# Two small products turned round, and a modulation sum moved, in a ten-stage block on one core

## The chip, the cores and the metric

The kernel runs on one core of a Trainium2 chip. The metric is device time in microseconds (us). The engines are TensorE (PE; its weight loads are PEld), VectorE (DVE), ScalarE (ACT), GpSimd (POOL, unused here) and SyncE (SP), which issues most DMAs.

## The reference, cut to what matters

A sequence of 256 tokens of width 1024 goes through ten stages: ffn, mamba, ffn, ffn, moba, ffn, sb, cffn, dsa, cffn. Each begins with an RMSNorm whose shift, scale and gate come from a vector product with the condition `c` (adaLN):

```python
m = c_act @ w + b
shift, scale, gate = jnp.split(m, 3, axis=-1)
h = rmsnorm(x, g) * (1.0 + scale[:, None, :]) + shift[:, None, :]
x = x + g * y
```

The Mamba stage needs, beside its wide projection, 32 columns of `h @ w_in`, one for each head: `dt = softplus(dt + dt_bias)`. Its cumulative sums set the decays between tokens. The sparse attention (dsa) needs 8 columns of `h @ w_in`, the weights `wi` of the index heads; a token's index score is the sum over heads of `wi` times the relu of a product of index query and index key, and the best 256 keys are kept.

## The kernel before

`x` is kept transposed in SBUF, 8 tiles of 128 channels x 256 tokens. Everything is computed at better than one-pass precision: each operand is split into a part rounded to a short format (`w_hi`, `h_hi`, type fp32r) and the rest (`w_lo`, `h_lo`), and `three` issues three matmuls, hi x hi, hi x lo and lo x hi (L1365 to L1367). Weights come as 277 blocks of 128x2048. For each block SyncE loads `raw` (a ring of six), ScalarE rounds it to `w_hi` (L420) and VectorE subtracts (`w_lo`, L816); these two are called `split`, and they run two blocks ahead of TensorE. A block is used up by `gemm` (48 products of 256 columns into one PSUM bank: two halves `m` of 24) or by `gemm_out` and `last` (into the accumulators, banks 0 to 3).

Each engine has its own program, a hand-written order of instructions; engines wait for one another only through counted semaphores, `k.wait(name, stage)` and `k.inc(name, instruction)`. A waiting instruction holds back all that stands behind it on its engine.

The small weights, 8 tiles of 128x40 (32 columns for Mamba, 8 for dsa), are in `ws_hi` and `ws_lo`. In the Mamba stage TensorE does, for the first group of heads: the first block into bank 4; `timestep`; the second block into bank 5 (B and C); the third into bank 7 (z); `cum` (L1517 to L1523, the cumulative sums of dt x a); then transposes and scores. `timestep` has h as weights (128 channels x 128 tokens) and the 32 small columns as moving operand: 2 halves of tokens x 8 tiles x 3 products, 48 in all. The result stands with tokens on partitions, as VectorE's `timestep` (L1055 to L1071, softplus) wants it, in bank 6, columns 0 to 63. VectorE has before it in its queue a `split` and the conv taps of the first block (L1095); ScalarE does four of the steps in between (L538 to L543).

In dsa `sparse_front` does: the block of latent and index keys into bank 4; 48 products with 8 columns into bank 7; the product for the relative bias (`relp`, L1765) into bank 7; two more blocks (index queries) into banks 5 and 6, with a ones product for a norm between them (L1772); two transposes (L1775); then index scores for eight heads (L1782, L1783), which VectorE sums with the `wi` weights (L1308). VectorE's copy `relv` (L1294) lets ScalarE store the bias and go on to its next `split`.

The adaLN sums: during earlier ffn stages VectorE has multiplied and summed the modulation weights (`gather`, `fold`). At a stage's end `last` does the last block in four pairs of tiles. After each pair VectorE's `residual` adds to `x` (L949, and for Mamba L945 before it; a `split` stands between pairs 1 and 2), ScalarE squares (L436), and TensorE sums the squares over partitions for the next norm (`squares`, L1423, fp32, two passes each). `modulation` on TensorE (L1415, one product of 96 columns with the `fold` matrix) stands between `squares` 1 and 2 of the tail; `modulation` on VectorE (four sums L874 and two or three small steps, L886 to L889) stands behind `residual`. The next norm waits for `rstd` and for it (L907).

Of the kernel before, what the change touches and what calls it, by code (L numbers as in the profile page):

```python
# [23 lines left out]
ALU = mybir.AluOpType  # L24
# [3 lines left out]
P = 128  # L28
T = 256
# [93 lines left out]
class Plan:  # L123
# [20 lines left out]
    def steps(self, st, kind):  # L144
        g = GROUPS[kind]
        out = {"fold": 4, "mods": 1, "modv": 1, "pair": 3, "xup": 8, "sq": 8, "ss": 1, "ln": 1, "rstd": 1,
               "t": 8, "hhi": 8, "hlo": 8, "zero": 1, "ahi": 0, "alo": 0}
        if st == RESCALED:
            out |= {"sq": 16, "ln": 2, "rstd": 2, "ms2": 4, "xfin": 8}
        if kind in ("ffn", "cffn"):  # L150
            out |= {"silu": g, "mul": g, "ahi": g, "alo": g}
        if kind == "cffn":
            out |= {"cid": 2 * g, "tap1": 2 * g, "tap2": 2 * g}
        if kind == "mamba":
            out |= {"dtp": 1, "dta": 12, "dtx": 4, "acp": 1, "acv": 3, "sq0": 1, "cid": 2 * g, "tap": 6 * g,
                    "sil": 3 * g, "acg": g, "xt": g, "cb": g, "br": 4 * g, "xdt": g, "cbs": g, "dx": g,
                    "dec": 4 * g, "wv": 4 * g, "yc": g, "y1": g, "zw": g, "yz": g, "ysq": g, "yn": g, "yac": g,
                    "ahi": g, "alo": g, "rs2p": 1, "rs2": 2, "xr": 8}
        if kind in ("moba", "sb", "dsa"):
            out |= {"sc": 4 * g, "qev": g, "lg": 4 * g, "ptp": 4 * g, "ptc": 4 * g, "pv": 2 * g,  # L160
                    "ahi": 2 * g, "alo": 2 * g}
        if kind in ("moba", "sb"):
            out |= {"kev": g, "vev": g}
        if kind in ("moba", "dsa"):
            out |= {"mx": 4 * g, "nm": 4 * g, "ex": 4 * g, "rc": 4 * g, "prs": 4 * g}
        if kind == "sb":
            out |= {"ab": 4 * g, "ea": 4 * g, "la": 4 * g, "lk": 4 * g, "prb": 4 * g, "arg": 4 * g}
        if kind == "dsa":
            out |= {"qev2": g, "pre": 3, "wip": 1, "relp": 1, "wiv": 1, "relv": 1, "ix": 8, "rel": 8,
                    "isc": 10, "top": 32, "msk": 2, "ksq": 1, "kss": 1, "klr": 2, "gkq": 1, "kn": 1,  # L170
                    "ltp": 1, "ltc": 1, "qsq": 2 * g, "qss": g, "qlr": 2 * g, "ol": 2 * g, "olc": 2 * g, "wu": g}
        return out
# [35 lines left out]
def build(nc, weights, mods, params, consts, xin, out, stages=None):  # L208
# [3 lines left out]
    with ExitStack() as ctx:  # L212
# [94 lines left out]
        dta = mix[:, 5696:5824].rearrange("p (a d h) -> p a d h", a=2, d=2)  # L307
        ea = mix[:, 5824:5856]
        r2 = mix[:, 5856:6112]
        yn = work[:, 1536:2048].rearrange("p (a t) -> p a t", a=2)  # L310

        Q = view(0, 4, T)
# [484 lines left out]
        def _(eng):  # L797
# [242 lines left out]
            def mamba(st):  # L1040
# [2 lines left out]
                step = [0]  # L1043

                def timestep():
                    k.wait("dtp", st)

                    def dt_step(ins, wait=True):
                        k.inc("dta", ins)
                        step[0] += 1  # L1050
                        if wait:
                            k.wait("dta", st, b=step[0] - 1)


                    dt_step(eng.tensor_tensor(dv.rearrange("p (a h) -> p a h", a=2),  # L1055
                                              bank[6][:, 0:64].rearrange("p (a h) -> p a h", a=2),
                                              par_("dtb").unsqueeze(1).to_broadcast([P, 2, 32]), ALU.add), False)
                    k.wait("dtx", st, b=1)
                    dt_step(eng.tensor_scalar(dw, de, 1.0, None, ALU.add))
                    k.wait("dtx", st, b=2)  # L1060
                    dt_step(eng.tensor_scalar(dw, dw, 1.0, None, ALU.subtract))
                    dt_step(eng.tensor_scalar(dm, dw, 0.0, None, ALU.is_equal))
                    dt_step(eng.tensor_tensor(dw, dw, dm, ALU.add))
                    dt_step(eng.reciprocal(dw, dw))
                    dt_step(eng.tensor_tensor(dl, dl, dm, ALU.add))
                    dt_step(eng.tensor_tensor(dl, dl, dw, ALU.mult))
                    dt_step(eng.tensor_tensor(dl, dl, de, ALU.mult))
                    dt_step(eng.scalar_tensor_tensor(out=dtt, in0=dv, scalar=0.0, in1=dl, op0=ALU.max, op1=ALU.add))
                    k.wait("dtx", st, b=3)
                    for d in range(2):  # L1070
                        dt_step(eng.scalar_tensor_tensor(  # L1071
                            out=dta[:, :, d, :], in0=dtt.rearrange("p (a h) -> p a h", a=2),
                            scalar=-1.0, in1=ea.unsqueeze(1).to_broadcast([P, 2, 32]), op0=ALU.mult, op1=ALU.mult), False)
# [214 lines left out]
            def sparse_front(st):  # L1288

                split(st, b=0)  # L1290
                k.wait("relp", st)
                k.inc("wiv", eng.tensor_scalar(wi, bank[7][:, 0:16].rearrange("p (a h) -> p a h", a=2), 8 ** -0.5,
                                               None, ALU.mult))
                k.inc("relv", eng.tensor_copy(relS, bank[7][0:16, P:512]))  # L1294
                k.inc("gkq", eng.tensor_tensor(gkq, par_("qn"), par_("kn"), ALU.mult))
                k.inc("isc", eng.memset(isc, 0.0))
                split(st, b=1)
                k.wait("gkq", st)
                k.wait("klr", st, b=1)
                k.inc("kn", eng.scalar_tensor_tensor(out=kn, in0=latT, scalar=gkq, in1=rstd[:, :],  # L1300
# [44 lines left out]
            for st, kind in enumerate(stages):  # L1345
                norm(st)
                programs[kind](st)
                residual(st)
                if st + 1 < NST:
                    modulation(st + 1)  # L1350


        @block.tensor
        def _(eng):
# [11 lines left out]
                eng.matmul(dst, ah, bl, start=False, stop=False, skip_group_check=skip)  # L1366
                return eng.matmul(dst, al, bh, start=False, stop=stop, skip_group_check=skip)  # L1367

            def gemm(dst, st, i=0, a=0, b=0, tokens=False, first=False):

                hi, lo = [w.rearrange("p (k n) -> p k n", k=KT) for w in begin(st, i, a, b)]
                both = [(m, slice(m * P, (m + 1) * P), dst[:, m * T:(m + 1) * T]) for m in range(2)]
# [13 lines left out]
                                            skip_group_check=True)  # L1386
                else:
                    for m, part, d in both:
                        for kk in range(KT):
                            if tokens:  # L1390
                                mm = three(d, h_hi[:, kk, part], h_lo[:, kk, part], hi[:, kk, :], lo[:, kk, :],
                                           kk == 0, kk == KT - 1)
                            else:
                                mm = three(d, hi[:, kk, part], lo[:, kk, part], h_hi[:, kk, :], h_lo[:, kk, :],
                                           kk == 0, kk == KT - 1)
# [75 lines left out]
            def last(st, ready):  # L1471
# [6 lines left out]
                if st == 0:  # L1478
                    eng.wait_ge(sems["go"], KT + 2)
                    eng.matmul(bank[7][:, 96:128], con_("fold"), gfold, start=True,  # L1480
                               stop=True).then_inc(sems["gmods"], 1)
                for pair in range(4):
                    if pair == 3 and more:
                        squares(st + 1, 0)
# [8 lines left out]
                        mm.then_inc(sems["blk"], 1)  # L1493
                if more:
                    squares(st + 1, 1)
                    modulation(st + 1)
                    squares(st + 1, 2)
                    squares(st + 1, 3)

            def mamba(st):  # L1500
                def timestep():
                    k.wait("rstd", st)
                    for tt in range(2):
                        for kk in range(KT):
                            part = slice(tt * P, (tt + 1) * P)
                            ws = slice(40 * kk, 40 * kk + 32)
                            mm = three(bank[6][:, 32 * tt:32 * tt + 32], h_hi[:, kk, part], h_lo[:, kk, part],
                                       ws_hi[:, ws], ws_lo[:, ws], kk == 0, kk == KT - 1)
                    k.inc("dtp", mm)

                tri, ones = con_("tri"), con_("ones")
# [57 lines left out]
                def body(i, a, b):  # L1569
# [5 lines left out]
                    else:  # L1575
                        timestep()
                    k.wait("cbs", st, i, 1, -1)
                    gemm(bank[5], st, i, a, b + 1)
                    if more:
                        y_out(i)  # L1580
                        k.wait("dec", st, i, 4, -1)
# [173 lines left out]
            def sparse_front(st):  # L1755
                gemm(bank[4], st, b=0, first=True)
                k.wait("modv", st)
                for tt in range(2):
                    for kk in range(KT):
                        part, ws = slice(tt * P, (tt + 1) * P), slice(40 * kk + 32, 40 * kk + 40)  # L1760
                        mm = three(bank[7][:, 8 * tt:8 * tt + 8], h_hi[:, kk, part], h_lo[:, kk, part],
                                   ws_hi[:, ws], ws_lo[:, ws], kk == 0, kk == KT - 1)
                k.inc("wip", mm)
                o, _ = PARAMS["relb"]
                k.inc("relp", eng.matmul(bank[7][0:16, P:512], par[0:32, o:o + 16], con_("onehot", 32),  # L1765
                                         start=True, stop=True))
                for n in (1, 2):
                    gemm(bank[4 + n], st, b=n)
                    if n == 1:
                        k.wait("relv", st)  # L1770
                        k.wait("ksq", st)
                        k.inc("kss", eng.matmul(bank[7][:, 0:T], con_("ones"), qsq[0][:, 0:T], start=True, stop=True))  # L1772
# [131 lines left out]
```

## Time and profile before

| what | us |
|---|---|
| runs | 1894.99, 1885.89, 1892.75; median 1892.75 |
| profiled execution, its own time | 1896.41 |
| its span from first to last instruction | 1894.6 |
| TensorE matmuls busy | 1795.6 (95%) |
| TensorE weight loads busy | 1737.1 (92%) |
| VectorE busy | 1445.1 (76%) |
| ScalarE busy | 961.7 (51%) |
| mean granted TensorE clock | 0.982 |

Matmuls are pipelined: each record is longer than the distance to the next start, so a pace is read from the starts. A granted clock of 1.00 is 2.4 GHz, 0.50 is 1.2 GHz.

### The profile page before, as it was taken

How to read it: one execution, taken by the hardware profiler on the slowest of the kernel's cores; microseconds unless marked ns; L12 is line 12 of the kernel's file. 1: busy time of each engine (PE TensorE's matmuls, PEld its weight loads, DVE VectorE, ACT ScalarE, POOL GpSimd, SP SyncE). 2: the span in 40 equal slices, each digit the busy share in tenths (PEclk: the TensorE clock that was granted, in tenths of full speed). 3: DMA queues.
4: the chain of work that ended last, by engine and by line, in shares of the span. 5: the costliest groups of instructions: out<-in, count | busy, mean ns of one | idle time of the engine just before them, and what ended most of it. 6: DMA issues, size and time to landing. Idle time of an engine off the chain costs nothing.

```text
span 1894.6 us, 34144 instructions
## 1 busy us (share of the span) xinstructions
PE 1795.6 (95%) x14644; PEld 1737.1 (92%) x14644; DVE 1445.1 (76%) x1716; ACT 961.7 (51%) x1256; POOL 0.2 (0%) x4
## 2 busy tenths in 40 slices
PE   2998999999999999999989999898999999989999
PEld 2998989998999999999979999897999988979999
DVE  7799877877789878976548897655898667447666
ACT  3433456666543454346564444555644555666553
POOL 0000000000000000000000000000000000000000
PEclk9999999999999999999999999999999998999999
DMA  9998824343599759973426996232485544324551
GB/s 399 417 366 340 300 109 156 135 177 134 187 380 365 309 218 371 361 296 130 178 101 262 347 393 250 109 140 109 175 320 192 181 142 161 118 90 162 193 180 42
DMA packets 67278, 426.11 MB, mean 225 GB/s; under 512 B 7264, under 2 KB 10352, under 8 KB 30448
## 3 DMA queue, kind: packets, MB, share of 16 engines
q1 hardware_dynamic: 63216, 415.21, 57.9%
q10 hardware_dynamic: 3968, 9.63, 1.5%
q8 instruction: 61, 1.00, 0.2%
q14 instruction: 33, 0.27, 0.0%
HBM read 423.74 MB, written 3.17 MB: 225 GB/s over the span
## 4 chain that ended last, share of the span: by engine, by line
PE 85%; DVE 10%; ACT 3%; issue 1%; DMA 1%; SPq 0%; DVEq 0%; ACTq 0%
PE bank L1365 24%; PE bank L1367 24%; PE bank L1366 24%; DVE w_lo L816 3%; PE bank L1423 2%; DVE macc L847 2%; DMA modws<-mods 1%; PE bank L1687 1%; PE bank L1378 1%; PE bank L1380 1%; DVE mix L1002 1%; PE bank L1385 1%; PE bank L1529 1%; PE bank L1668 1%; PE bank L1564 0%
## 5 line engine op out<-in xcount | busy, mean ns | idle before, releaser
L1365 PE MATMUL bank<-h_hi,w_hi 128*128 128x256 f32 x2864 | 810.4, 283 | 14.0 <-DVE w_lo L816 12.3
L1366 PE MATMUL bank<-h_lo,w_hi 128*128 128x256 f32 x2864 | 804.4, 281 | 0.0
L1367 PE MATMUL bank<-h_hi,w_lo 128*128 128x256 f32 x2864 | 804.2, 281 | 0.0
L816 DVE TENSOR_TENSOR w_lo<-raw,w_hi 128x2048 fp32r<-128x2048 f32 x277 | 633.4, 2288 | 128.1 <-ACT w_hi L420 127.6
L420 ACT ACTIVATE w_hi<-raw 128x2048 fp32r<-128x2048 f32 x277 | 529.3, 1911 | 155.8 <-PE bank L1367 144.5
L1365 PEld LDWEIGHTS bank<-h_hi,w_hi 128*128 128x128 f32 x2864 | 543.8, 190 | 19.5 <-DVE w_lo L816 15.1
L1366 PEld LDWEIGHTS bank<-h_lo,w_hi 128*128 128x128 f32 x2864 | 546.7, 191 | 0.2
L1367 PEld LDWEIGHTS bank<-h_hi,w_lo 128*128 128x128 f32 x2864 | 545.3, 190 | 0.0
L1365 PE MATMUL bank<-a_hi,w_hi 128*128 128x256 f32 x1280 | 362.4, 283 | 3.1 <-DVE a_lo L1244 3.1
L1366 PE MATMUL bank<-a_lo,w_hi 128*128 128x256 f32 x1280 | 359.6, 281 | 0.0
L1367 PE MATMUL bank<-a_hi,w_lo 128*128 128x256 f32 x1280 | 359.2, 281 | 0.0
L1365 PEld LDWEIGHTS bank<-a_hi,w_hi 128*128 128x128 f32 x1280 | 241.7, 189 | 6.0 <-issue 5.2
L1366 PEld LDWEIGHTS bank<-a_lo,w_hi 128*128 128x128 f32 x1280 | 241.6, 189 | 0.2
L1367 PEld LDWEIGHTS bank<-a_hi,w_lo 128*128 128x128 f32 x1280 | 241.7, 189 | 0.0
L847 DVE SCALAR_TENSOR_TENSOR macc<-modws,cact,macc 128x1536 f32<-128x1536 f32 x126 | 226.3, 1814 | 0.0
L1002 DVE SCALAR_TENSOR_TENSOR mix<-bank,par,mix 128x254 f32<-128x254 f32 (+1 forms) x176 | 76.7, 478 | 49.5 <-ACT mix L495 47.9
L470 ACT ACTIVATE a_hi<-mix 128x512 fp32r<-128x512 f32 x40 | 25.3, 633 | 154.1 <-PE bank L1367 124.8
L456 ACT ACTIVATE mix<-bank 128x512 f32<-128x512 f32 x44 | 26.4, 600 | 121.5 <-PE bank L1367 121.5
L495 ACT ACTIVATE mix<-bank,par 128x256 f32<-128x256 f32 x88 | 44.8, 559 | 84.0 <-PE bank L1367 83.9
L1423 PE MATMUL bank<-work,con 128*128 128x256 f32 x160 | 42.9, 399 | 32.2 <-DMA con<-consts 31.2
L1423 PEld LDWEIGHTS bank<-work,con 128*128 128x128 f32 x160 | 29.7, 200 | 36.1 <-DMA con<-consts 31.2
L968 DVE TENSOR_TENSOR a_lo<-mix,a_hi 128x512 fp32r<-128x512 f32 x40 | 27.7, 692 | 42.1 <-ACT a_hi L470 42.1
(250 smaller groups left out, 1692.4 us busy)
## 6 DMA issues: line engine op xcount, KB each, us to landing
raw<-weights SPq DMA_DIRECT2D x277, 1024.0 KB, 4.9
modws<-mods SPq DMA_DIRECT2D x144, 768.0 KB, 6.5
mix<-mods SPq DMA_DIRECT2D x6, 1024.0 KB, 8.1
mix<-mods ACTq DMA_DIRECT2D x8, 512.0 KB, 10.3
modws<-mods SPq DMA_DIRECT2D x2, 1024.0 KB, 12.1
biases<-scratch ACTq DMA_DIRECT2D x1, 2048.0 KB, 12.2
mix<-biases ACTq DMA_DIRECT2D x4, 512.0 KB, 4.2
par<-params ACTq DMA_DIRECT2D x1, 1189.0 KB, 8.3
```

What stands on the lines that cost most here:

```text
L420: eng.activation(w_hi[g % NW][:, :], raw[g % NRAW][:, :], ACT.Copy).then_inc(sems["whi"], 1)
L456: k.inc("silu", eng.activation(sg, bank[4][:, :].rearrange("p (a t) -> p a t", a=2), ACT.Silu))
L470: k.inc("ahi", eng.activation(z_hi if final else a_hi[:, :, :], act, ACT.Copy))
L495: ins = eng.activation(dst[:, m, :], b[:, m * T:(m + 1) * T], ACT.Identity, scale=cw(i, t, 2), bias=cw(i, t, 3))
L816: eng.tensor_tensor(w_lo[g % NW][:, :], raw[g % NRAW][:, :], w_hi[g % NW][:, :], ALU.subtract).then_inc(sems["wlo"], 1)
L847: ins = eng.scalar_tensor_tensor(out=m, in0=modw[q % 4], scalar=c, in1=m, op0=ALU.mult, op1=ALU.add)
L968: k.inc("alo", eng.tensor_tensor(z_lo if final else a_lo[:, :, :], act, z_hi if final else a_hi[:, :, :], ALU.subtract))
L1002: ins = eng.scalar_tensor_tensor(out=dst[:, m, lag:T], in0=b[:, m * T:(m + 1) * T - lag], scalar=cw(i, 22 * up + m, tap), in1=dst[:, m, la ...
L1365: eng.matmul(dst, ah, bh, start=start, stop=False, skip_group_check=skip)
L1366: eng.matmul(dst, ah, bl, start=False, stop=False, skip_group_check=skip)
L1367: return eng.matmul(dst, al, bh, start=False, stop=stop, skip_group_check=skip)
L1423: mm = eng.matmul(bank[6][:, r * T:(r + 1) * T], con_("ones"), (sq2 if r else work3)[:, m, :], start=m == r == 0, stop=m == KT - 1, skip_g ...
```

## The change

Three edits. The Mamba time step has the small columns as weights and h as moving operand: 8 x 3 = 24 products of 256 columns give 32 rows (heads) x 256 tokens; VectorE copies them to SBUF (`dtrow`, semaphores `dtr`, `dtc`); two transposes on TensorE, put between the two halves of the second block, bring them back to tokens on partitions, in bank 6 from column 256 on. The index weights of dsa are done likewise: 24 products give 8 rows in bank 6, VectorE copies them (`wirow`), two transposes stand behind the second block, and the scaled copy `wi` (`wiv`) moves behind VectorE's second split; the third block, which writes bank 6, waits for it. `modulation` of the next stage moves, on TensorE from the tail to the head of `last` (behind `ready`), and on VectorE ahead of `residual`.

```diff
@@ VectorE, Mamba
                 def timestep():
+                    k.wait("dtr", st)
+                    k.inc("dtc", eng.tensor_copy(dtrow, bank[6][0:32, 0:T]))
                     k.wait("dtp", st)
...
-                                              bank[6][:, 0:64].rearrange("p (a h) -> p a h", a=2),
+                                              bank[6][:, T:T + 64].rearrange("p (a h) -> p a h", a=2),
@@ VectorE, sparse_front
                 split(st, b=0)
+                k.wait("wir", st)
+                k.inc("wic", eng.tensor_copy(wirow, bank[6][0:8, 0:T]))
                 k.wait("relp", st)
-                k.inc("wiv", eng.tensor_scalar(wi, bank[7][:, 0:16].rearrange("p (a h) -> p a h", a=2), 8 ** -0.5,
-                                               None, ALU.mult))
...
                 split(st, b=1)
+                k.wait("wip", st)
+                k.inc("wiv", eng.tensor_scalar(wi, bank[6][:, T:T + 16].rearrange("p (a h) -> p a h", a=2), 8 ** -0.5,
+                                               None, ALU.mult))
@@ VectorE, stages
                 programs[kind](st)
-                residual(st)
                 if st + 1 < NST:
                     modulation(st + 1)
+                residual(st)
@@ TensorE, gemm
                     for m, part, d in both:
+                        if m and between:
+                            between()
@@ TensorE, last
+                if more:
+                    modulation(st + 1)
                 for pair in range(4):
...
                 if more:
                     squares(st + 1, 1)
-                    modulation(st + 1)
                     squares(st + 1, 2)
@@ TensorE, Mamba
                 def timestep():
                     k.wait("rstd", st)
+                    for kk in range(KT):
+                        ws = slice(40 * kk, 40 * kk + 32)
+                        mm = three(bank[6][0:32, 0:T], ws_hi[:, ws], ws_lo[:, ws], h_hi[:, kk, :], h_lo[:, kk, :],
+                                   kk == 0, kk == KT - 1)
+                    k.inc("dtr", mm)
+
+                def timestep_columns():
+                    k.wait("dtc", st)
                     for tt in range(2):
-                        for kk in range(KT):
-                            part = slice(tt * P, (tt + 1) * P)
-                            ws = slice(40 * kk, 40 * kk + 32)
-                            mm = three(bank[6][:, 32 * tt:32 * tt + 32], h_hi[:, kk, part], h_lo[:, kk, part],
-                                       ws_hi[:, ws], ws_lo[:, ws], kk == 0, kk == KT - 1)
+                        mm = eng.transpose(bank[6][:, T + 32 * tt:T + 32 * tt + 32], dtrow[:, tt * P:(tt + 1) * P],
+                                           con_("ident")[0:32, 0:32])
                     k.inc("dtp", mm)
...
-                    gemm(bank[5], st, i, a, b + 1)
+                    gemm(bank[5], st, i, a, b + 1, between=None if more else timestep_columns)
@@ TensorE, sparse_front
-                for tt in range(2):
-                    for kk in range(KT):
-                        part, ws = slice(tt * P, (tt + 1) * P), slice(40 * kk + 32, 40 * kk + 40)
-                        mm = three(bank[7][:, 8 * tt:8 * tt + 8], h_hi[:, kk, part], h_lo[:, kk, part],
-                                   ws_hi[:, ws], ws_lo[:, ws], kk == 0, kk == KT - 1)
-                k.inc("wip", mm)
+                for kk in range(KT):
+                    ws = slice(40 * kk + 32, 40 * kk + 40)
+                    mm = three(bank[6][0:8, 0:T], ws_hi[:, ws], ws_lo[:, ws], h_hi[:, kk, :], h_lo[:, kk, :],
+                               kk == 0, kk == KT - 1)
+                k.inc("wir", mm)
...
                 for n in (1, 2):
+                    if n == 2:
+                        k.wait("wiv", st)
                     gemm(bank[4 + n], st, b=n)
                     if n == 1:
+                        k.wait("wic", st)
+                        for tt in range(2):
+                            mm = eng.transpose(bank[6][:, T + 8 * tt:T + 8 * tt + 8], wirow[:, tt * P:(tt + 1) * P],
+                                               con_("ident")[0:8, 0:8])
+                        k.inc("wip", mm)
                         k.wait("relv", st)
```

`dtrow` is `work[0:32, 1536:1792]` and `wirow` is `work[0:8, 0:256]`.

## Rows read from the trace of the kernel before

**Rows 1.** The page: span, and the chain that ended last by engine.
```profile
span 1894.6 us, 34144 instructions
...
PE 85%; DVE 10%; ACT 3%; issue 1%; DMA 1%; SPq 0%; DVEq 0%; ACTq 0%
```
**Rows 2.** Timeline of PE, Mamba stage: start us, duration us, what.
```profile
246.57 0.26 PE L1366 MATMUL bank<-ws_lo,h_hi 128*128 128x32 f32 x1
...
250.70 0.33 PE L1367 MATMUL bank<-ws_hi,h_lo 128*128 128x32 f32 x1
...
252.78 0.56 PE L1365 MATMUL bank<-h_hi,w_hi 128*128 128x256 f32 x1
...
257.73 0.28 PE L1367 MATMUL bank<-h_hi,w_lo 128*128 128x256 f32 x1
...
265.90 0.28 PE L1367 MATMUL bank<-h_hi,w_lo 128*128 128x256 f32 x1
```
**Rows 3.** Windows: stretch, length, busy us (records) of PE, PEld, DVE, ACT, POOL, clock, DMA.
```profile
246.50:250.80 4.30, 4.30 (x41) 4.30 (x40) 4.20 (x7) 1.02 (x2) 0.00 (x0) 1.00 0.19 38
252.80:257.40 4.60, 4.60 (x22) 4.60 (x23) 3.14 (x13) 3.85 (x6) 0.00 (x0) 0.50 0.04 16
283.50:286.70 3.20, 3.20 (x32) 2.79 (x31) 2.65 (x6) 2.82 (x3) 0.00 (x0) 1.00 0.37 113
1543.70:1547.70 4.00, 4.00 (x39) 4.00 (x38) 1.77 (x1) 1.07 (x3) 0.00 (x0) 1.00 0.35 66
1551.60:1554.40 2.80, 2.80 (x14) 2.80 (x14) 1.07 (x4) 1.61 (x1) 0.00 (x0) 0.50 0.04 9
```
**Rows 4.** Timeline of DVE, Mamba stage: taps, first and last softplus step, a copy from PSUM.
```profile
248.78 2.69 DVE L1095 SCALAR_TENSOR_TENSOR mix<-bank,par,mix 128x255 f32<-128x255 f32 x6
252.98 0.23 DVE L1055 TENSOR_TENSOR mix<-bank,par 128x64 f32<-128x64 f32 x1 [1.52 <-PE bank L1367]
...
256.75 0.36 DVE L1071 SCALAR_TENSOR_TENSOR mix<-mix 128x64 f32<-128x64 f32 x2
...
267.74 0.41 DVE L1080 CAST acg<-bank 64x256 fp32r<-64x256 f32 x1
```
**Rows 5.** Timeline of PE, dsa front: first and last small product, bias product, next block.
```profile
1543.74 0.17 PE L1365 MATMUL bank<-ws_hi,h_hi 128*128 128x8 f32 x1
...
1549.91 0.35 PE L1367 MATMUL bank<-ws_hi,h_lo 128*128 128x8 f32 x1
1550.19 1.46 PE L1765 MATMUL bank<-con,par 32*16 32x384 f32 x2
1551.58 0.58 PE L1365 MATMUL bank<-h_hi,w_hi 128*128 128x256 f32 x1
```
**Rows 6.** Timeline of PE, dsa front: the ones product in fp32 and two transposes.
```profile
1558.59 0.59 PE L1772 MATMUL bank<-work,con 128*128 128x256 f32 x2
...
1564.67 0.38 PE L1775 MATMUL bank<-con,mix 128*128 128x128 f32 x2
```
**Rows 7.** Timeline of DVE, dsa front: the copy of the bias and the next split.
```profile
1551.78 0.53 DVE L1294 COPY mix<-bank 16x384 f32<-16x384 f32 x1
...
1554.73 2.29 DVE L816 TENSOR_TENSOR w_lo<-raw,w_hi 128x2048 fp32r<-128x2048 f32 x1 [1.95 <-ACT w_hi L420]
```
**Rows 8.** Timeline, end of the fourth stage (ffn): squares, modulation, next norm.
```profile
863.37 1.02 PE L1423 MATMUL bank<-work,con 128*128 128x256 f32 x4
...
864.23 0.36 PE L1415 MATMUL bank<-folded,con 128*128 128x96 f32 x2
...
864.43 1.92 PE L1423 MATMUL bank<-work,con 128*128 128x256 f32 x8
864.63 0.75 DVE L874 TENSOR_TENSOR modv<-bank,par 32x24 f32<-32x24 f32 x4
...
867.34 0.88 DVE L907 SCALAR_TENSOR_TENSOR work<-x,gs,rstd 128x256 f32<-128x256 f32 x2 [1.55 <-ACT rstd L426]
```
**Rows 9.** Timeline of PE, end of the Mamba stage: the last squares.
```profile
483.23 1.13 PE L1423 MATMUL bank<-work,con 128*128 128x256 f32 x4 [0.69 <-ACT work L436]
...
484.69 1.13 PE L1423 MATMUL bank<-work,con 128*128 128x256 f32 x4 [0.32 <-ACT work L436]
```

More of the change, by code:

```diff
@@ L154, in steps @@
         if kind == "mamba":
-            out |= {"dtp": 1, "dta": 12, "dtx": 4, "acp": 1, "acv": 3, "sq0": 1, "cid": 2 * g, "tap": 6 * g,
+            out |= {"dtr": 1, "dtc": 1, "dtp": 1, "dta": 12, "dtx": 4, "acp": 1, "acv": 3, "sq0": 1, "cid": 2 * g, "tap": 6 * g,
                     "sil": 3 * g, "acg": g, "xt": g, "cb": g, "br": 4 * g, "xdt": g, "cbs": g, "dx": g,
@@ L168, in steps @@
         if kind == "dsa":
-            out |= {"qev2": g, "pre": 3, "wip": 1, "relp": 1, "wiv": 1, "relv": 1, "ix": 8, "rel": 8,
+            out |= {"qev2": g, "pre": 3, "wir": 1, "wic": 1, "wip": 1, "relp": 1, "wiv": 1, "relv": 1, "ix": 8, "rel": 8,
                     "isc": 10, "top": 32, "msk": 2, "ksq": 1, "kss": 1, "klr": 2, "gkq": 1, "kn": 1,
@@ L309, in build @@
         r2 = mix[:, 5856:6112]
+        dtrow, wirow = work[0:32, 1536:1792], work[0:8, 0:256]
         yn = work[:, 1536:2048].rearrange("p (a t) -> p a t", a=2)
@@ L1367, in three, with gemm @@
                 return eng.matmul(dst, al, bh, start=False, stop=stop, skip_group_check=skip)
-            def gemm(dst, st, i=0, a=0, b=0, tokens=False, first=False):
+            def gemm(dst, st, i=0, a=0, b=0, tokens=False, first=False, between=None):
                 hi, lo = [w.rearrange("p (k n) -> p k n", k=KT) for w in begin(st, i, a, b)]
```

## The prediction

> **What bounds the kernel now.** I read the page first: the chain that ended last is matmul for 85% of a span of 1894.6 us [rows 1]. So a microsecond taken out of TensorE's stream counts in full wherever TensorE is the last to arrive, and the views that matter are TensorE's timeline at the places that the diff touches, then the granted clock there (windows), then VectorE and ScalarE around them, to see whether they can follow an earlier TensorE.
>
> The diff touches two stretches of small products and the ends of nine stages. Both small stretches lie on the chain: TensorE has no gap in them. In the Mamba stage the 48 products with 32 columns start every (250.70 - 246.57) / 37 = 0.1117 us [rows 2], while the big products just behind them, with 256 columns, start every (265.90 - 257.73) / 72 = 0.1135 us at full clock [rows 2]. Eight times the columns at the same pace: what paces the small product is not its moving side; its 128x128 weight load is the only thing that it has in common with the big one. And the clock: it is granted in full up to 250.8 us, 1.00 in the windows view, and is at half from about 250.8 to 257.4 us, 0.50 [rows 3], that is 1.2 instead of 2.4 GHz, though TensorE was never idle. The same happens behind the 8-column products of the DSA stage, 1.00 until 1547.7 us and 0.50 in the stretch from 1551.6 us [rows 3]. What went before the fall both times is some 4 us of products that stream 32 or 8 columns in the time of 256.
>
> **Part one, Mamba time step.** Before, from 246.53 (one start ahead of the first row of [rows 2]) to the cumulative products at 266.01 (the last product starts at 265.90, one pace before them [rows 2]): 19.48 us. These are 48 small products, 6.25 us, of which 48 x 0.1117 = 5.36 is the pace and 0.89 the low clock; and 96 big ones, 13.23 us from 252.78, of which 96 x 0.1135 = 10.90 is the pace and 2.33 the low clock.
>
> After: 24 products with 256 moving columns of h and 32 weight columns. No row shows so narrow a weight in this number format. From below, the 256 columns are streamed in any case, so 0.1135 us each; from above, an fp32 product of 256 columns: the two squares at a stage's end, two records each, fill 863.37 to 864.23, 0.43 us a product [rows 8]. I take 0.1135, as both sides are rounded to the short format exactly as in the big products: 24 x 0.1135 = 2.72 us. Two transposes come in: the two 128x128 ones of rows 6 take 0.38 us with the tail of the last, some 0.11 apart; I take 0.25 for both, 0.38 as the bound. The 96 big products stay: 10.90 if the clock holds. Sum 13.87.
>
> The new wait: TensorE needs the evacuated row product (dtc) after half of the second block, at 246.53 + 2.72 + 24 x 0.1135 = 251.97 us. VectorE does the first conv taps until 248.78 + 2.69 = 251.47 [rows 4], then the copy; the nearest row is the 64x256 copy from PSUM, 0.41 us [rows 4]; ready at about 251.9. So a stall of 0 to 0.1 us, I take 0.05. Behind the waiting TensorE stand the other half of that block and the z block. VectorE's chain of small steps began at 252.98 and took until about 257.1 [rows 4], 4.1 us; it now begins at about 252.4 and ends at 256.5, while the cumulative products that wait for it come at 246.53 + 13.92 = 260.45. Hidden by 4 us. ScalarE's second SiLU is the tightest follower: conv of B and C now waits for its own queue (time step, split, table, SiLU) until about 257.5, VectorE's taps end at 261.5, SiLU at 262.2, and TensorE wants it after the cumulative products (1.5 us) and the transposes (0.5), at 262.4. So nothing is lost there, but with 0.2 us to spare. Gain 19.48 - 13.92 = 5.6 us, 3.2 of it clock.
>
> The Trainium skill speaks against this edit in TensorE: Matmul & The Clock Gate, section Back-to-back issue gap: small products may start as close as about 25 ns. By that floor the 48 would cost 1.2 us and the 24 long ones, at the pace above, 2.7, a loss of 1.5 us in each stage. The trace disagrees for this stream, 0.1117 us a start; the same page's section LDWEIGHTS, columns over 1.2 GHz, 107 ns for 128, is what the row follows.
>
> **Part two, index weights.** Before, 1543.74 to 1564.67 [rows 5, 6]: 20.93 us. After: 2.72 for 24 products; the relative-bias product 1551.58 - 1550.19 = 1.39 at half clock [rows 5], so 0.70 at full; the qi block 48 x 0.1135 = 5.45 instead of 7.01 (1551.58 to 1558.59); transposes 0.25; the ones product 0.43; the last block as before, from the end of the ones product at 1558.59 + 0.43 to 1564.67, 5.65 [rows 6]. With 0.1 for the new waits, 15.3. Gain 5.6 us, 3.35 of it clock (1.09 in the small products, 0.69, 1.56).
>
> Waits here: the last block now waits for wiv, since it overwrites the bank. wiv stands behind VectorE's split on its queue, which stands behind ScalarE's split, which waits for the copy relv. In the trace that runs from 1551.58 to the end of VectorE's split at 1554.73 + 2.29 = 1557.02 [rows 5, 7], 5.44 us after the bias product. After the change the bias product ends at 1547.2, the split at 1552.6, the transposes at 1552.9: just in time, and wiv (0.17 us) and its signals are covered by the 0.43 us product. If the cover is gone, it costs what VectorE is late. The sparse chain behind (index scores, top-k, mask) starts from TensorE's results and moves with them.
>
> **Part three, modulation.** One product per stage end moves from between the squares to the head of the last block. At a usual end the tail shows it as 864.43 - 864.23 = 0.20 us [rows 8] in an unbroken stream; the squares it delays are ready. At the head it costs the same 0.2, as it stands behind the wait for the activations. Eight ends: about nothing. VectorE's six small steps (0.75 us for the four, 1.2 in all) ended at 865.8, while the norm that needs them waited until 867.34 for rstd [rows 8]: they were hidden, and before the first residual pair (12 products, 1.4 us) they are hidden again. At the Mamba end the tail is paced by VectorE, TensorE waits 0.69 and 0.32 us for squares [rows 9], so nothing is gained behind; the head runs at half clock and starts the residual chain 0.4 us later. One other head (moba) may run at half clock, 0.2. Loss 0.6 us in all; between 0 and 2 (nine ends x 0.2).
>
> **Sum.** -5.6 - 5.6 + 0.6 = -10.6 us. The profiled execution took 1896.41 us around its 1894.6 span, 3.7 above the median of the three runs, 1892.75; I set the difference against the median: 1882.2 us, 0.56% faster. A difference under 0.5%, 9.5 us, is what a measurement of this kernel can hardly tell from none.
>
> **Rivals.** (A, 0.66) as summed, its own range 1879 to 1886: other stretches at half clock, such as behind the one-column products, may shift by a few microseconds.
>
> (B, 0.14) the clock falls all the same, or fell for another reason. For it: 32 and 8 weight columns leave most of the array idle, and no row has the like. Against: the output products of Mamba with 64 weight columns ran at clock 1.00 (283.50 to 286.70) [rows 3]. Only the pace is gained: 11.2 - 6.55 = 4.65, less 0.6: 1888.7; with one fall of two, 1885.4. Beside it stands the Trainium skill, TensorE: Matmul & The Clock Gate, section "What's actually happening": the gate follows how busy the engine has been. Read as no idle gaps, it would grant full clock before and after and leave the same 1888.7; the trace disagrees, as the fall came in an unbroken stream.
>
> (C, 0.04) the other side: narrow weights run at the fp32 pace, 0.43 us. Then 48 x 0.316 = 15.2 us come back: 1897.4, slower than before. It decides from 0.1135 + 10.6 / 48 = 0.33 us a product on.
>
> (D, 0.08) the waits bite: VectorE reaches the Mamba copy or wiv only after a split, 2.2 us late in one or both: 1884.4 to 1886.6.
>
> (E, 0.08) the earlier arrival is given back behind, in other low clocks or at a wait that I don't see: 1888 to 1893, rarely above.
>
> **Numbers.** 1882.2, range 1878 to 1890: A, B and D, and the lower part of E; C and the worst of E are left out. Faster by over 0.5% means under 1883.3, which cuts through A: 0.53. Within: 0.42. Slower by over 0.5%, only C or E with something worse: 0.05.
>
> **What would show it.** Right: 24 products on the small weights per stage, 0.11 us apart; clock 1.00 from there to the cumulative products; those 13.9 us after the first small product (19.5 before); 15.3 us in place of 20.9 in DSA; no wait of TensorE above 0.2 us for dtc and wiv; stage ends unchanged within 0.4 us. Wrong: half clock after the row products, starts 0.2 us or more apart at full clock, TensorE waiting for a VectorE split, or a later stage longer by what was gained.

## The result, and the profile after

The changed kernel takes 1881.36 us, median of 20 runs (1874.69 to 1888.04); the kernel before, in 20 runs beside them, 1891.02 (1881.76 to 1895.39). Ratio 0.9954, 95% interval 0.9941 to 0.9967: faster by 0.46%, 8.7 us (6.2 to 11.2). (The two medians alone differ by 9.7 us; all sizes below go by the ratios with their intervals.) The forecast was 10.6 us, 0.56%, in a range of 1878 to 1890 us. The likeliest case came, a little smaller than summed. The prediction gave 0.53 to a gain over 0.5% and 0.42 to a smaller one; the measured value lies in the second, and the interval does not settle it.

The page, to set beside [rows 1]:

```profile
span 1878.9 us, 34059 instructions
...
PE 84%; DVE 10%; ACT 3%; issue 2%; DMA 1%; SPq 0%; DVEq 0%; ACTq 0%
```

The two profiled spans differ by 15.7 us, nearly twice the measured gain, so the profile is read place by place here and not by its ends. First TensorE's timeline in the Mamba stage, to set beside [rows 2]:

```profile
249.20 0.28 PE L1371 MATMUL bank<-h_hi,ws_hi 128*32 128x256 f32 x1
...
251.98 0.28 PE L1371 MATMUL bank<-h_hi,w_hi 128*128 128x256 f32 x1
...
254.60 0.28 PE L1373 MATMUL bank<-h_hi,w_lo 128*128 128x256 f32 x1
254.81 0.30 PE L1521 MATMUL bank<-con,work 32*128 32x32 f32 x2
255.04 0.38 PE L1371 MATMUL bank<-h_hi,w_hi 128*128 128x256 f32 x1
255.26 0.28 PE L1372 MATMUL bank<-h_lo,w_hi 128*128 128x256 f32 x1
...
263.51 0.28 PE L1373 MATMUL bank<-h_hi,w_lo 128*128 128x256 f32 x1
263.63 0.31 PE L1531 MATMUL bank<-mix,con 128*128 128x32 f32 x2
```

The 24 row products take 251.98 - 249.20 = 2.78 us, 0.116 a start; the two transposes stand in the middle of the second block, and the cumulative products start 263.63 - 249.20 = 14.43 us after the first small product, where it was 19.48. Then the windows of the changed kernel (columns as in [rows 3]): the row products and what follows them, in Mamba and in dsa.

```profile
249.20:251.90 2.70, 2.70 (x26) 2.52 (x24) 2.70 (x4) 1.02 (x2) 0.00 (x0) 1.00 0.00 0
252.00:263.60 11.60, 11.60 (x100) 11.43 (x99) 9.34 (x24) 7.33 (x10) 0.00 (x0) 1.00 0.35 111
1538.60:1541.40 2.80, 2.80 (x26) 2.01 (x23) 1.72 (x1) 1.08 (x3) 0.00 (x0) 1.00 0.18 23
1541.50:1554.10 12.60, 12.60 (x103) 11.76 (x103) 6.65 (x8) 5.21 (x5) 0.00 (x0) 1.00 0.63 229
```

The clock is 1.00 (2.4 GHz) in all four windows, where [rows 3] had 0.50 behind both sets of small products. VectorE around the new wait, to set beside [rows 4]: the taps, the copy, the first softplus step.

```profile
251.33 2.67 DVE L1098 SCALAR_TENSOR_TENSOR mix<-bank,par,mix 128x255 f32<-128x255 f32 x6
253.91 0.40 DVE L1048 COPY work<-bank 32x256 f32<-32x256 f32 x1
255.15 0.22 DVE L1058 TENSOR_TENSOR mix<-bank,par 128x64 f32<-128x64 f32 x1 [0.83 <-PE bank L1521]
```

The copy ends at 254.31, 0.4 us before TensorE is through with the first half of the block: no stall. And TensorE in the dsa front, to set beside [rows 5, 6]:

```profile
1538.60 0.28 PE L1371 MATMUL bank<-h_hi,ws_hi 128*8 128x256 f32 x1
...
1541.29 0.28 PE L1373 MATMUL bank<-h_hi,ws_lo 128*8 128x256 f32 x1
1541.50 0.81 PE L1778 MATMUL bank<-con,par 32*16 32x384 f32 x2
...
1547.90 0.28 PE L1787 MATMUL bank<-con,work 8*128 8x8 f32 x2
1548.11 0.70 PE L1792 MATMUL bank<-work,con 128*128 128x256 f32 x2
1548.46 0.47 PE L1371 MATMUL bank<-h_hi,w_hi 128*128 128x256 f32 x1
...
1554.11 0.38 PE L1795 MATMUL bank<-con,mix 128*128 128x128 f32 x2
```

1554.11 - 1538.60 = 15.51 us, where it was 20.93. The last block starts right behind the ones product; wiv holds nobody up.

### The profile page after: what moved, and what is told of

Same layout as the page of the kernel before. It is cut to its first block, busy times and chain, and to the rows that moved or that the text cites. A ratio compares the mean times of both kernels' runs of the same rounds, so it can differ in the third digit from the quotient of the medians.

```text
span 1878.9 us, 34059 instructions
## 1 busy us (share of the span) xinstructions
PE 1780.6 (95%) x14600; PEld 1720.5 (92%) x14600; DVE 1445.2 (77%) x1718; ACT 961.7 (51%) x1256; POOL 0.2 (0%) x4
## 4 chain that ended last, share of the span: by engine, by line
PE 84%; DVE 10%; ACT 3%; issue 2%; DMA 1%; SPq 0%; DVEq 0%; ACTq 0%
PE bank L1371 24%; PE bank L1373 24%; PE bank L1372 24%; DVE w_lo L817 3%; PE bank L1431 2%; DVE macc L848 1%; DMA modws<-mods 1%; PE bank L1701 1%; PE bank L1384 1%; PE bank L1386 1%; DVE mix L1003 1%; PE bank L1391 1%; PE bank L1543 1%; PE bank L1682 1%; DVE mix L828 1%
```

## Experiments

The times of one and the same kernel spread by 13 to 20 us (before: 1881.81 to 1902.01 in 35 runs), so the intervals below are some 4 us to each side, and the sizes are read from the traces, one of each kernel. All ratios are to the kernel before on the same chip.

**Mamba alone.** The whole change without the turned index weights and without the move of modulation.

```diff
 before, Mamba timestep (TensorE)
-  48 products: weights h (128x128), moving 32 columns of ws
+  24 products: weights ws (128x32), moving 256 columns of h; copy; two transposes
```

> Only the Mamba time step is turned; index weights and modulation as before. Theory 1 (pace and clock): the stretch from the first small product to the cumulative products takes 14.4 us instead of 19.5, clock 1.00 in it, the dsa stretch keeps its half clock; the kernel is 5 us faster (ratio 0.9973). Theory 2 (the low clock there had nothing to do with the small products): half clock still appears within the stretch, and the kernel is 2.4 us faster (0.9987).

Measured: 1889.31 us median, ratio 0.9982 (0.9959 to 1.0005). The windows, Mamba from the first small product to the cumulative ones, then dsa from the first small product to the transposes:

```profile
250.60:265.00 14.40, 14.40 (x124) 14.03 (x123) 12.22 (x27) 8.34 (x12) 0.00 (x0) 1.00 0.27 86
1540.20:1561.10 20.90, 20.90 (x150) 19.57 (x149) 7.97 (x8) 6.18 (x8) 0.00 (x0) 0.84 0.44 152
```

The turned stretch is 14.45 us at clock 1.00, the other one 20.90 at 0.84, as before. Theory 1 holds in the trace; the ratio's interval has both theories in it, and no effect at all.

**Index weights alone.** The same for dsa only.

```diff
 before, sparse_front (TensorE)
-  48 products: weights h, moving 8 columns of ws, bank 7
+  24 products: weights ws (128x8), moving 256 columns of h, bank 6; copy; two transposes behind block 1
```

> Only the index weights are turned; Mamba and modulation as before. Theory 1: from the first small product to the two latent transposes 15.5 us instead of 20.9, clock 1.00 in it, the Mamba stretch as before at 19.5; the kernel 5.4 us faster (0.9971). Theory 2: half clock still appears there, 2.2 us faster (0.9988).

Measured: 1888.62 us, ratio 0.9984 (0.9966 to 1.0002). The windows, Mamba and dsa:

```profile
246.40:266.30 19.90, 19.90 (x146) 19.90 (x146) 12.54 (x27) 9.08 (x13) 0.00 (x0) 0.83 0.32 106
1542.70:1558.50 15.80, 15.80 (x128) 14.07 (x126) 8.37 (x9) 6.29 (x8) 0.00 (x0) 1.00 0.56 195
```

The mirror image: the untouched Mamba stretch 19.84 us at 0.83, the turned dsa stretch 15.89 at 1.00. That is 0.38 us more than in the changed kernel, with the clock at 1.00 in both: the two big blocks in it start 0.120 and 0.122 us apart on average here, 0.116 and 0.118 there. The last section comes back to this pace.

**Modulation alone.**

```diff
 TensorE, last
+                if more:
+                    modulation(st + 1)
                 for pair in range(4):
...
                     squares(st + 1, 1)
-                    modulation(st + 1)
 VectorE
                 programs[kind](st)
-                residual(st)
                 if st + 1 < NST:
                     modulation(st + 1)
+                residual(st)
```

> Only modulation is moved. Theory 1: the product costs at the head what it saves in the tail, and the Mamba end starts its residual chain 0.4 us later: 0 to 0.6 us slower (1.0000 to 1.0003). Rival: the tails get shorter by 0.2 us each and the heads hide it, 1.8 us faster (0.9990). Second rival: the move costs about 2 us (1.0011), which would be why the change measured 8.7 us and not 10.6.

Measured: 1889.88 us, ratio 0.9988 (0.9966 to 1.0010): the runs exclude neither no effect nor a gain of 1.8 us, and the second rival's loss (1.0011) lies only just outside. The stage ends say more. In the trace of this kernel the eight usual ends go from the first squares to the first step of rstd (L424) in 5.07 us (8.53 in the one with double squares), where they took 5.26 to 5.31 (8.75), and start their last block's products 0.14 to 0.22 us behind the modulation product. What the tail saves the head costs.

The same trace shows that the stretch in the Mamba stage, which this edit leaves alone, isn't a fixed number. The windows, small products and what follows them:

```profile
245.90:250.00 4.10, 4.10 (x35) 4.10 (x34) 4.03 (x7) 1.02 (x2) 0.00 (x0) 0.88 0.22 32
250.00:260.00 10.00, 10.00 (x51) 10.00 (x51) 5.87 (x15) 4.60 (x7) 0.00 (x0) 0.54 0.23 93
```

Here the low clock came earlier and stayed longer, and the stretch took 21.09 us, against 19.48 in the kernel before and 19.84 with the index weights alone. What turning the Mamba products gains so lies between 5.0 and 6.7 us, by the execution that it is set against.

**Both turned, modulation as before.** The change less the diff just shown.

> Both small stretches turned, modulation as before. Theory 1: 10.5 us faster than before (0.9944), that is 0 to 0.6 us faster than the whole change. If the move of modulation costs 2 us, this kernel is faster than the whole change by that; if it gains 1.8, slower by that.

Measured: 1880.60 us, ratio 0.9934 (0.9912 to 0.9957), Mamba 14.43 us and dsa 15.89 at clock 1.00. The whole change is at 0.9954 (0.9941 to 0.9967); the intervals overlap, so whether the move of modulation costs or gains anything the runs can't tell, and the turned products alone reach the whole gain.

**The same 48 products, made wide.** Is it the few streamed columns that bring the clock down? h stays the weights, and each product streams 256 columns of small weights, of which 32 are used.

```diff
-                            ws = slice(40 * kk, 40 * kk + 32)
-                            mm = three(bank[6][:, 32 * tt:32 * tt + 32], h_hi[:, kk, part], ...
+                            ws = slice(40 * kk, 40 * kk + 256)
+                            mm = three(bank[6][:, T * tt:T * tt + T], h_hi[:, kk, part], ...
```

> The kernel before, its 48 Mamba products with h as weights kept, but each streams 256 columns of small weights instead of 32 (the other 224 are not used). dsa and modulation as before. If it is the few streamed columns that bring the clock down: clock 1.00 through the stretch, 48 starts 0.1135 us apart (5.45 us instead of 6.25), cumulative products 16.4 us after the first small product (19.5 before): all of the clock gain, 3.2 us, and none of the pace gain. If it is the stage, the count or the weight reloads: half clock again, 19.5 us or more.

Measured: 1890.84 us, ratio 1.0002 (0.9983 to 1.0021). The runs show no gain; one of 2.9 us, 0.9985, lies just inside the interval, so that the gain is read from the trace alone. TensorE's timeline, and the windows of the small products and of the two blocks behind them:

```profile
248.01 0.28 PE L1365 MATMUL bank<-ws_hi,h_hi 128*128 128x256 f32 x1
...
253.57 0.28 PE L1367 MATMUL bank<-ws_hi,h_lo 128*128 128x256 f32 x1
...
264.58 0.30 PE L1517 MATMUL bank<-mix,con 128*128 128x32 f32 x2
```
```profile
248.00:253.60 5.60, 5.60 (x50) 5.60 (x49) 4.91 (x8) 1.02 (x2) 0.00 (x0) 1.00 0.38 116
253.70:264.50 10.80, 10.80 (x98) 10.80 (x97) 7.66 (x19) 8.08 (x11) 0.00 (x0) 1.00 0.34 135
```

Same place, same number of products and of weight loads, eight times the columns: the small products take (253.57 - 248.01) / 47 = 0.118 us each, the clock never falls there, and the stretch is 16.57 us instead of 19.48, 2.9 us less. The wide products themselves are slower than the 0.1117 us of [rows 2] by 48 x 0.0066 = 0.3 us, so the clock's share is 3.2 us, as summed (0.89 + 2.33). In dsa, left as it was, the clock still fell (0.84 over 20.92 us).

**The 48 products in two runs of 24.**

```diff
-                        timestep()
+                        timestep(0)                      # first half of the tokens
                     k.wait("cbs", st, i, 1, -1)
-                    gemm(bank[5], st, i, a, b + 1)
+                    gemm(bank[5], st, i, a, b + 1, between=None if more else lambda: timestep(1))
```

> The kernel before, its 48 Mamba products in two runs of 24, the second between the halves of the second block. dsa and modulation as before. If the fall needs one long run of small products: clock 1.00, cumulative products 16.4 us after the first. If what counts is how much of it comes within a longer time: half clock again, about 19.5 us.

Measured: 1889.65 us, ratio 0.9997 (0.9973 to 1.0020). The windows: small and big products up to the end of the second run, behind it, and the rest.

```profile
247.30:255.20 7.90, 7.90 (x73) 7.90 (x71) 4.90 (x8) 1.02 (x2) 0.00 (x0) 1.00 0.37 135
255.30:259.10 3.80, 3.80 (x22) 3.80 (x22) 2.27 (x10) 2.95 (x6) 0.00 (x0) 0.58 0.00 0
259.30:265.20 5.90, 5.90 (x54) 5.90 (x54) 5.10 (x10) 4.80 (x6) 0.00 (x0) 1.00 0.36 121
```

Neither expectation came. The clock still falls, behind the second run of 24, but for about half as long (17.98 us for the stretch, against 19.48). In this one trace splitting the run is half a cure; with the length of the fall as variable as it was above, one trace does not show that it always is.

**The row products three times over.** In the changed kernel, 72 instead of 24 in each stage; the first two sets are computed and thrown away.

```diff
-                    for kk in range(KT):
+                    for kk in 3 * list(range(KT)):
```

> The changed kernel with each set of 24 row products, in Mamba and in dsa, issued three times over (72 products, the first two sets thrown away). If narrow weights alone also bring the clock down when the run is long: half clock within or behind the 72 products. My theory: clock 1.00 throughout, starts 0.1135 to 0.118 us apart, both stretches longer by 48 x 0.115 = 5.5 us (Mamba 20.0, dsa 21.0), since only the streamed columns count.

Measured once: 1886.38 us. That is one run, too little to compare; it is only 5 us above the changed kernel's median, where the two stretches in its trace are 5.6 and 5.9 us longer. The windows: the 72 products and what follows, Mamba, then dsa.

```profile
245.30:253.60 8.30, 8.30 (x74) 7.67 (x72) 4.72 (x8) 1.02 (x2) 0.00 (x0) 1.00 0.41 128
253.70:265.30 11.60, 11.60 (x100) 11.43 (x99) 7.49 (x19) 7.33 (x10) 0.00 (x0) 1.00 0.09 17
1538.70:1547.00 8.30, 8.30 (x74) 6.25 (x72) 1.76 (x1) 1.08 (x3) 0.00 (x0) 1.00 0.36 128
1547.10:1560.10 13.00, 13.00 (x103) 12.15 (x103) 6.65 (x8) 5.21 (x5) 0.00 (x0) 1.00 0.44 151
```

Over 8 us of products with 32 and with 8 weight columns, longer than any run of small products before, and the clock stays at 1.00. Narrow weights don't bring it down. The stretches are 20.05 and 21.37 us (expected: 20.0 and 21.0).

**Modulation ahead of the wait.** The one place where the move could still win: in front of the waits at the head of the last block.

```diff
             def last(st, ready):
+                more = st + 1 < NST
+                early = st > 0 and stages[st] in ("ffn", "cffn")
+                if more and early:
+                    modulation(st + 1)
...
-                if more:
+                if more and not early:
                     modulation(st + 1)
```

> The changed kernel with TensorE's modulation product ahead of the wait for the last block's weights and activations, in the ffn and cffn stages but the first (five ends). If TensorE waits there anyway, the product is hidden: from the last product of the block before to the next rstd 0.2 us less at each such end, 1 us in all (0.9995 of the changed kernel), which runs cannot tell; the trace can. If TensorE doesn't wait there, nothing.

Measured: 1879.03 us, ratio 0.9936 (0.9914 to 0.9958). The edit touches four ends (the expectation says five, but the last stage has no modulation after it). TensorE waits at the head in one of them only, the first cffn stage:

```profile
1523.00 0.36 PE L1423 MATMUL bank<-folded,con 128*128 128x96 f32 x2
1524.18 0.36 PE L1371 MATMUL bank<-h_hi,w_hi 128*128 128x256 f32 x1 [0.82 <-DVE h_lo L1023]
```

In the ffn stages the block's products start 0.14 us behind the modulation product, with or without this edit. So it hides 0.2 us once. Of the three kernels at 0.9934 to 0.9954 no one can be called the best by these runs.

## Why the prediction was right, point by point

**The clock.** Shown. In the ten traces the small products with few streamed columns were left in nine times, counting the two runs of 24 as one (both stages of the kernel before and of the one with modulation alone, one or both in four others), and each time the clock fell to half within them or behind them. Turned or made wide they stand eleven times, and it never fell within the stretch. The same products made wide keep their place, their number and their weights, and 72 products with narrow weights change nothing. Rival B is out, and the row that spoke against it, the output products with 64 weight columns at clock 1.00, was the right one to go by.

The mean granted clock of all runs agrees in direction and roughly in size. A stretch at half clock lowers the mean by half its length. On one chip the mean is 0.9847 over 35 runs of the kernel before and 0.9890 over the 12 with both sets turned and modulation as before: 0.0043 x 1885 = 8.1 us given back. On the other it is 0.9859 over 25 and 0.9885 over the 8 of the last experiment: 4.9 us. The prediction had 6.55.

**The pace.** Shown: 0.116 and 0.117 us a start for the row products against 0.1135 taken. Rival C, the fp32 pace of 0.43, is out. The 25 ns floor of the Trainium skill (TensorE: Matmul & The Clock Gate, section Back-to-back issue gap) would have made the change a loss; that section gives it for matmuls by themselves and says that the weight loads of a stream count too, and the prediction rightly went by the 0.1117 us of [rows 2]. That the weight load sets this pace is argued, not shown: products with 8 and with 32 streamed columns start 0.112 us apart alike, and with 256 columns narrow weights are no faster than full ones, but no run here has narrow weights and few columns together.

**The terms that were mis-sized.** Mamba gained 19.48 - 14.43 = 5.05 us, not 5.6. The row products took 2.78 instead of 2.72. The transposes delayed the second half by 0.43 us (the second product of that half at 255.26, where 254.60 + 2 x 0.1135 = 254.83 would be due), not by 0.30. And the 70 starts from there to 263.51 are 0.118 us apart, not 0.1135, 0.3 us more. This last is no chance of one trace: in all five kernels with these transposes the big products start 0.1135 us apart before them and 0.118 behind them. The prediction took the pace of the unchanged blocks for granted. dsa gained 5.42, not 5.6: the row products with the way to the bias product took 2.90 instead of 2.72, the bias product 0.74 instead of 0.70, the first big block 5.66 instead of 5.45, while the transposes and the ones product took 0.12 less than summed, and the 0.1 for waits was not needed. Together 10.5 against 11.2.

**The waits.** Rival D is out: VectorE had the Mamba copy ready 0.4 us early, and the last dsa block started without a gap. ScalarE's SiLU of B and C, the tightest follower in the prediction, was ready in time, too: TensorE's last scores (L1544 before, L1558 after) start 2.41 us behind the cumulative products in both kernels.

**Modulation.** The tail got 0.22 us shorter and the head 0.14 to 0.22 longer at each usual end. From the last product ahead of the block to rstd (L426, in the changed kernel L427) the eight ends together give back less than 0.1 us in the changed kernel and 0.2 with modulation alone. At the Mamba end the timeline of the changed kernel shows the product at half clock and VectorE's own sums hidden behind it:

```profile
470.51 0.58 PE L1423 MATMUL bank<-folded,con 128*128 128x96 f32 x2
471.13 0.75 DVE L875 TENSOR_TENSOR modv<-bank,par 32x24 f32<-32x24 f32 x4 [2.54 <-PE bank L1423]
```

From the last product ahead of it to rstd this end took 13.87 us, 13.03 in the kernel before. Not all of that is the move, as the clock was low for longer. The windows, the kernel before, the changed one, and the one with both sets turned and modulation as before:

```profile
473.33:486.36 13.03, 12.01 (x72) 10.39 (x70) 9.14 (x24) 6.79 (x13) 0.00 (x0) 0.90 0.23 80
```
```profile
470.08:483.95 13.87, 12.78 (x72) 10.97 (x70) 9.32 (x24) 6.80 (x13) 0.00 (x0) 0.84 0.22 76
```
```profile
467.17:480.78 13.61, 12.68 (x72) 11.06 (x70) 9.23 (x24) 6.79 (x13) 0.00 (x0) 0.84 0.22 77
```

At the same clock, 0.84, the move costs 0.26 us. Predicted a loss of 0.6 in all, read 0.1 to 0.2.

**The sum.** Read from the traces: 5.05 + 5.42 - 0.2 = 10.3 us. The runs say 8.7, 6.2 to 11.2, and the two are consistent. Rival E, that a part is given back behind, can be looked for from one rstd to the next. The whole Mamba stage took 247.18 us before (239.19 to 486.36) and 242.10 after (241.85 to 483.95), 5.1 less, as much as its stretch (its end took 0.84 us more, as just shown, and the part between 0.87 less). The dsa stage took 166.36 before (1536.39 to 1702.75) and 155.89 after (1531.25 to 1687.14), 10.5 less; 5.05 of it lies behind the stretch, where the clock was 0.93 before and 0.96 after, and that is the larger part of what the two profiled spans differ by beyond the change. In the kernels with dsa as before, time lost to half clock there goes from 1.7 to 10.2 us, with dsa turned from 3.4 to 5.1, so these traces don't show that it belongs to the change. So in this pair of traces nothing is given back within the two stages; in others the pace of the last section moves a stage by as much as 5 us, and a small loss behind can't be excluded.

**What was luck.** The measured 1881.36 us lies 0.8 us from the forecast of 1882.2, nearer than the gain does (8.7 against 10.6), because the kernel before came out at 1891.02 and not at the 1892.75 that the forecast started from. And the range of 1878 to 1890 holds the time of rival B as well, 1888.7: it is the traces that tell the mechanism, not the time.

## What to carry to other kernels

Products with 8, 32 or 256 streamed columns, each with weights of its own, all cost 0.11 to 0.12 us a start here at full clock, so count the products and not the multiplications: put the small matrix on the weight side and let the long one stream, if a copy and a transpose can be hidden. Look at the granted clock behind a run of small products as well: here over half of the gain was the clock, and most of that (2.33 + 0.69 + 1.56 of 6.55 us by the prediction's terms, which the traces bear out) was in the products that came after the run. Moving a short instruction along an engine that does not wait gives nothing; look for the wait first.

## What the runs showed of the hardware that was not expected

The pace of the big products has two values at full clock. In the second ffn stage the same loop took 187.78 us from rstd to rstd in the kernel before and 192.92 with both sets turned and modulation left alone, at clock 1.00 in both. The windows, the kernel before first:

```profile
500.00:660.00 160.00, 160.00 (x1398) 160.00 (x1397) 142.67 (x89) 66.90 (x50) 0.00 (x0) 1.00 0.90 349
```
```profile
500.00:660.00 160.00, 160.00 (x1357) 160.00 (x1357) 139.27 (x87) 64.51 (x48) 0.00 (x0) 1.00 0.89 344
```

1398 products against 1357 in the same 160 us, 0.1144 and 0.1179 us each; short windows give 0.1133 or 0.1178 and little between. In the kernel before, the products with h as weights run at the faster value and those with a at the slower one; in the other kernel all run at the slower. Of the ten traces three have the slow kind of this stage (192.6 to 192.9 us), six the fast (187.8) and one lies between (189.05), and the stage has no change of this case in it. In the Mamba stage the value changes at the two transposes. What sets it stays open; it wasn't tried. With the stretches at half clock it may be part of why one kernel's runs differ by 13 to 20 us, which is not shown, with one trace of each kernel; in the trace it is as large as the effect of one of the edits.
